# The joint stage of a decoder layer: down sweeps over four token tiles and half the columns, decode steps placed anew, norms once per block

## The reference

```python
p = x @ w_in                                  # q | k | v | forget logits | pooling channels
att  = softmax(q.k/sqrt(d) + c[t] - c[s]) v   # c = cumulative log sigmoid of the forget gates, 8 heads x 64
pool = (trailing mean over 2/4/8/16 - u) @ w_pool * pool_scale
x1 = layer_norm(ALPHA * x + concat(att, pool) @ w_out)
h  = x1 @ w_up + b_up                         # 1024 -> 2 x 2816
hc = b_conv + sum_j h[t-2+j] * w_conv[j]      # causal, width 3, over positions
x2 = layer_norm(ALPHA * x1 + (gelu(hc[:, :2816]) * hc[:, 2816:]) @ w_down)
```

## Time and profile before

| | us |
|---|---|
| median of 3 runs | 3484.64 (3484.43 to 3485.49) |
| profiled execution | 3479.7 |
| its span | 3478.0 |
| joint stage, first up half to last down half | 1313 to 3289 |
| TensorE busy over the span | 3072.4 (88%) |
| VectorE, ScalarE, GpSimd busy | 2131.0, 1707.8, 723.0 |

### The profile page before, as it was taken

One profiled execution on the slowest core, in us unless ns is written; L12 is line 12 of the kernel. 1 busy time (PEld: TensorE's weight loads), 2 busy tenths in 40 slices (PEclk: granted clock), 3 DMA queues, 4 the chain that ended last, 5 costly groups with the idle time before them and its releaser, 6 DMA issues. The chain is left out here.

```text
span 3478.0 us, 57440 instructions
## 1 busy us (share of the span) xinstructions
PE 3072.4 (88%) x19568; PEld 2434.5 (70%) x19568; DVE 2131.0 (61%) x4159; ACT 1707.8 (49%) x3365; POOL 723.0 (21%) x1261
## 2 busy tenths in 40 slices
PE   5999956888887996999899999899998999999767
PEld 5999944776776875777666777677776677777533
DVE  4333434677775655766677566676666776655655
ACT  2111114666664113466446666456664556665445
POOL 0101010000000103233233343233342333322100
PEclk9999977999999998999999999899999999999979
DMA  4443464322203347677887677887777886757575
GB/s 164 127 127 119 119 167 124 71 71 63 68 18 105 125 147 229 206 235 251 284 306 241 219 261 237 284 288 241 247 259 258 298 280 233 255 191 263 180 286 202
DMA packets 287594, 682.11 MB, mean 196 GB/s; under 512 B 57335, under 2 KB 136855, under 8 KB 278815
## 3 DMA queue, kind: packets, MB, share of 16 engines
q1 hardware_dynamic: 191431, 365.36, 32.6%
q0 software_dynamic: 91840, 298.40, 25.1%
q10 hardware_dynamic: 4032, 14.68, 1.2%
HBM read 607.42 MB, written 71.53 MB: 195 GB/s over the span
## 5 line engine op out<-in xcount | busy, mean ns | idle before, releaser
L1436 PE MATMUL F_ps_u<-X_x_hi,F_w_hi 128*128 128x512 f32 x1408 | 579.1, 411 | 7.3 <-DVE F_w_lo L1664 7.3
L1437 PE MATMUL F_ps_u<-X_x_lo,F_w_hi 128*128 128x512 f32 x1408 | 558.2, 396 | 0.0
L1438 PE MATMUL F_ps_u<-X_x_hi,F_w_lo 128*128 128x512 f32 x1408 | 556.4, 395 | 0.0
L1664 DVE TENSOR_TENSOR F_w_lo<-X_raw,F_w_hi 128x512 fp32r<-128x512 f32 x470 | 318.1, 681 | 367.8 <-ACT F_w_hi L1572 367.3
L1572 ACT CAST F_w_hi<-X_raw 128x512 fp32r<-128x512 f32 x470 | 283.7, 613 | 267.6 <-PE F_ps_y L1438 102.5
L1864 POOL DMA_DIRECT2D F_kin<-cache_k x512 | 277.7, 542 | 554.7 <-DVE F_kt L1718 361.1
L1893 POOL DMA_DIRECT2D F_vin<-cache_v x512 | 281.9, 551 | 296.8 <-issue 172.8
L1436 PE MATMUL F_ps_y<-F_w_hi,F_g_hi 128*128 128x512 f32 x704 | 296.5, 421 | 48.9 <-DVE F_w_lo L1664 47.7
L1436 PEld LDWEIGHTS F_ps_u<-X_x_hi,F_w_hi 128*128 128x128 f32 x1408 | 269.4, 191 | 100.2 <-issue 34.8
L1718 DVE STREAM_TRANSPOSE F_kt<-F_kin 128x1024 f32<-128x1024 f32 x256 | 303.6, 1222 | 26.4 <-DMA F_kin<-cache_k 26.3
L1438 PEld LDWEIGHTS F_ps_u<-X_x_hi,F_w_lo 128*128 128x128 f32 x1408 | 268.5, 191 | 60.3
(11 more groups left out here) (291 smaller groups left out, 6070.4 us busy)
## 6 DMA issues: line engine op xcount, KB each, us to landing
F_kin<-cache_k POOLq DMA_DIRECT2D x512, 256.0 KB, 4.5
F_vin<-cache_v POOLq DMA_DIRECT2D x512, 256.0 KB, 4.4
X_raw<-w_up_t SPq DMA_DIRECT2D x118, 512.0 KB, 4.9
X_raw<-w_down SPq DMA_DIRECT2D x117, 512.0 KB, 5.7
F_raw<-w_down SPq DMA_DIRECT2D x59, 512.0 KB, 5.3
F_raw<-w_up_t SPq DMA_DIRECT2D x58, 512.0 KB, 5.2
S_raw<-w_up_t SPq DMA_DIRECT2D x22, 1024.0 KB, 10.3
sc_qk<-A_qk SPq DMA_DIRECT2D x16, 1024.0 KB, 5.1
```

What stands on the lines that cost most here:

```text
L1436: nc.tensor.matmul(out, a_hi, b_hi, start=first, stop=False)
L1437: nc.tensor.matmul(out, a_hi, b_lo, start=False, stop=False)
L1438: return nc.tensor.matmul(out, a_lo, b_hi, start=False, stop=last)
L1664: nc.vector.tensor_tensor(w_lo[:, q % 4, :], raw[q // 2 % RAW][:, q % 2 * 512:(q % 2 + 1) * 512], w_hi[:, q % 4, :].bitcast(F32), ALU.subt ...
```

## The change

- **Down sweep.** `SWEEPS` stays 2 but a sweep now takes all four token tiles (TPB) and one half of the columns. A down half is 4 tiles x 3 matmuls, and there are 44 of them in a block in place of 88. A load of w_down takes two row chunks and 512 columns (512 KB as before), 22 loads a block in place of 44. g is split 512 tokens wide, 44 times a block. The second sweep takes the chunks in the order 18 to 21, 0 to 17, so that the last four chunks of g are free for the second half of the residual (`rows[1]`).
- **Buffers.** A third split buffer of g lies over `h`. `forget` is halved: one unit per load, 64 KB, 256 loads in place of 128. `sums` moves into a kept area.
- **Decode placing.** `decode_places` in place of the list of slots. In an up part a unit starts at a multiple of four halves and takes three of them; in a down part its three steps lie on three consecutive halves. The last step lies on half 524 of 528; it was on 685 of 704.
- **Norms.** `BlockNorm`: the moments of the first column half are taken at the second sweep's start, those of the second at halves 1 and 3 of the next block, then one variance, one root and one inversion for the four rows, and the scaling of a row at halves 7, 9, 11 and 13 in four calls of 512 columns. Two stores a row.
- **Order.** ScalarE casts the weight half q + 4 inside `up_done`, ahead of the gelu. The loads of x are spread over the down part; the residual of a sweep waits tile by tile (`y_done`).

```diff
-    N, TPB, ST, RAW, UN, PARTS = TB, TB // P, 2, 3, NPG // 4, NPG // 4 + 1
-    KR = 3
-    SWEEPS = TPB // ST
-    UPH, DOWNH = 4 * FC, 2 * SWEEPS * FC
+    N, TPB, RAW, UN, PARTS = TB, TB // P, 3, NPG // 4, NPG // 4 + 1
+    KR, GR = 3, 3
+    SWEEPS = D // 512
+    UPH, DOWNH = 4 * FC, SWEEPS * FC
+    LATE = FC - TPB
...
+    def decode_places():
+        at, q = {}, 0
         for s in range(NB + 1):
+            names = ("Q", "R", None) if s == 0 else ("T", "E", "QV") if s < NB else ("T", "V")
             for u in range(UN):
+                if 0 < s and is_up(q):
+                    q += -(q % HB) % 4
+                for name in names:
+                    at[q] = (name, s if name in ("Q", "R", "QV") else s - 1, u)
+                    q += 1
+            if is_up(q):
+                q += -(q % HB) % 4
             for x in ((1, 2, 3, 4) if s < NB else (1, 2)):
+                at[q] = ("X", s, x)
+                q += 1
...
+        g_hi_h = nc.alloc_sbuf_tensor_at("F_g_hi_h", [P, N], F32R, offset=over_h)
+        rows = [r[:, :, :], g[:, LATE:FC, :]]
...
+        X_LOAD_AT, X_SPLIT_AT = (4, 7, 10, 13), (FC + 1, FC + 4, FC + 7, FC + 10)
+        R_LOAD_AT, R_LATE_AT = 15, FC + 8
+        MOMENTS_AT, ROOT_AT, SCALE_AT = (1, 3), 5, (7, 9, 11, 13)
...
+                    k = 2 * (i - 2 * FC)
+                    cols = slice(k // FC * 512, (k // FC + 1) * 512)
+                    src = io["w_down"][0, chunk(k) * P:(chunk(k) + 2) * P, cols].rearrange("(a p) c -> p a c", p=P)
...
+            def down_half(q, b, k):
+                pos, G, (hi, lo) = k % FC, SWEEPS * b + k // FC, g_split(k)
                 pe.wait_ge(lo_done, q + 1)
+                pe.wait_ge(g_lo_done, SWEEPS * FC * b + k + 1)
+                for i in range(TPB):
+                    if pos == 0 and G:
+                        pe.wait_ge(y_read, TPB * (G - 1) + i + 1)
                     toks = slice(i * P, (i + 1) * P)
+                    last = product(ps_y[:, i, :], hi[:, toks], lo[:, toks], w_hi[:, q % 4, :], w_lo[:, q % 4, :],
+                                   pos == 0, pos == FC - 1)
+                    if pos == FC - 1 and i + 1 < TPB:
+                        last.then_inc(y_done, 1)
...
                 nc.scalar.activation(cv[:, gv, :], h[:, gv, 0:N], ACT.Identity, bias=coef[:, f, gv, 4:5],
                                      scale=coef[:, f, gv, 1:2]).then_inc(tap0, 1)
+                if q + 4 < NQ:
+                    high(q + 4)
...
+    def scale_rows(self, dve, link, halves, k):
+        nc = self.nc
         dve.wait_ge(self.rows_in, 32)
+        for w, row in enumerate(halves):
+            last = nc.vector.scalar_tensor_tensor(row, row, self.mv[:, k, 0:1], self.gain[:, w * 512:(w + 1) * 512],
+                                                  ALU.subtract, ALU.mult)
+        link(last)
+        for w, row in enumerate(halves):
+            last = nc.vector.scalar_tensor_tensor(row, row, self.inv[:, k:k + 1], self.shift[:, w * 512:(w + 1) * 512],
+                                                  ALU.mult, ALU.add)
+        last.then_inc(self.gained, 1)
```

More of the change, by code:

```diff
@@ L1245, in __init__, with moments, variance @@
         self.rows_in, self.gained = m.sem("rows_in"), m.sem("gained")
         self.chain = m.sem("norm_chain")
-    def moments(self, dve, link, row, n, k):
+    def moments(self, row, w, k):
+        self.nc.vector.bn_stats(self.stats[:, k, w, :], row).then_inc(self.measured, 1)
+    def variance(self, dve, link, b):
         nc = self.nc
[L1250 to L1259, removed]
+        dve.wait_ge(self.measured, 2 * self.n * (b + 1))
+        for k in range(self.n):
+            aggr = nc.vector.bn_aggr(self.mv[:, k, :], self.stats[:, k, :, :].rearrange("p a b -> p (a b)"))
+            if k + 1 == self.n:
+                link(aggr)
@@ L1260, in scale_row, with take_root, invert @@
+        nc.vector.tensor_scalar(self.var[:, :], self.mv[:, :, 1], EPS, None, ALU.add).then_inc(self.var_ready, 1)
+    def take_root(self, act, b):
+        act.wait_ge(self.var_ready, b + 1)
+        self.nc.scalar.activation(self.root[:, :], self.var[:, :], ACT.Sqrt).then_inc(self.root_ready, 1)
+    def invert(self, dve, link, b):
         nc = self.nc
-        var, root, inv, t1 = (x[:, k:k + 1] for x in (self.var, self.root, self.inv, self.t1))
-        dve.wait_ge(self.root_ready, n + 1)
+        var, root, inv, t1 = (x[:, :] for x in (self.var, self.root, self.inv, self.t1))
+        dve.wait_ge(self.root_ready, b + 1)
@@ L1654, in _ @@
                         exp(s, 0)
-            for k in range(ST):
-                norm.take_root(act, TPB * BLOCKS - ST + k, k)
+            norm.take_root(act, BLOCKS - 1)
         @block.vector
@@ L1821, in _ @@
                         gate(b, FC - 1)
-                    if hf == 0 and f + 2 < SWEEPS * FC:
-                        rest_of_g(SWEEPS * FC * b + f + 2)
-                    if hf == 0 and f in X_SPLIT_AT and b + 1 < BLOCKS:
-                        rest_of_x(b + 1, 2 * X_SPLIT_AT.index(f))
-                    if sweep_end(q):
-                        residual(q)
-                for k in range(ST):
-                    if lag(q, 1 + k):
-                        measure(sweep_of(q - 1 - k), k)
-                    if lag(q, 2 + k):
-                        scale_row(sweep_of(q - 2 - k), k)
+                    if down(q) + 2 < SWEEPS * FC:
+                        rest_of_g(b, down(q) + 2)
+                    if down(q) in X_SPLIT_AT and b + 1 < BLOCKS:
+                        rest_of_x(b + 1, 2 * X_SPLIT_AT.index(down(q)))
+                    if down(q) % FC == FC - 1:
+                        residual(q, b, hf)
+                    if FC <= down(q) < FC + TPB:
+                        measure(b, 0, down(q) - FC)
+                if b and i in MOMENTS_AT:
+                    first = 2 * MOMENTS_AT.index(i)
+                    measure(b - 1, 1, first)
+                    measure(b - 1, 1, first + 1)
+                    if first + 2 == TPB:
+                        norm.variance(dve, norm_links, b - 1)
+                if b and i in SCALE_AT:
+                    if i == SCALE_AT[0]:
+                        norm.invert(dve, norm_links, b - 1)
+                    scale_rows(SCALE_AT.index(i))
                 if q in step_at:
@@ L1913, in _ @@
             for q in range(NQ):
-                for k in range(ST):
-                    if lag(q, 2 + k):
-                        finish(sweep_of(q - 2 - k), k)
+                i = q % HB
+                if q >= HB and i in SCALE_AT:
+                    finish(q // HB - 1, SCALE_AT.index(i))
                 if q in step_at:
```

251 lines of the change are left out of this document (120 added, 131 removed).

## The result

The changed kernel takes 3333.85 us (median of 4 runs, 3330.55 to 3335.91) against 3484.53 before: ratio 0.9567, 95% interval 0.9551 to 0.9584, 151 us less. Forecast were 3371 in a range of 3340 to 3430.

What follows compares the result with a forecast made beforehand. TensorE's matmuls took 1450 of the stage's 1976 us, plus decode units and near 200 of waits, with late w_down in down parts. Parts 301 + 3 x 300 + 3 x 166 + 158 = 1857, +5 at the end: 3371, range 3340 to 3430.

Steps and rivals of the forecast that it cites:

- the price of waits: Joint stage: allowances for waits at block starts and in down parts, 51 us in all.
- Rival D: Joint stage: all waits allowed for (51 us) are absent, 3320 us; chance 0.10.
- Matmuls and units: Down parts: matmuls 123.2 us, 13.3 decode units at 2.48 us, 3 between sequences: 159; last part 155 before waits.
- Up parts: Blocks 2 to 4: 21 groups at 13.27 us plus 14, 293, with allowance 300; first block 295, with allowance 301.
- Late pages: Down parts of blocks 1 to 3: 7 us each for late pages and the residual at a sweep's end; K landing in 5.1.
- The norms at a block start: Start of up parts: scaling, moments and rest of the norm fall into four groups; 7 us allowed, 6 in the first.
- The down part of before: Old down part: low weights late because ScalarE stood 25.8 us for w_down to land; 50.55 MB in 174 us.
- The score addition: Up parts: TensorE's 28 waits before transpose steps, 43.9 us, to go as two halves separate QK and transpose.
- The end: After the last matmul: residual, moments, root, inversion and scaling of four rows, +5 us, bounds +2 and +10.
- A: Down parts: the score-addition wait moves there, 41 units at 1.57 us, 64 us, giving 3435; chance 0.13.
- B: Down parts: transfers stay the bound, 46.4 MB at 244 GB/s, 24 us more three times, giving 3443; chance 0.09.
- C: Down parts: late K pages hold VectorE and then TensorE, 4.3 us a unit, 176 us, giving 3547; chance 0.04.

Runs made afterwards that it cites:

- e10: Changed kernel with the norm's small tiles allocated behind coef, so w_hi and x_hi both lie at 160 past a multiple of 256 bytes: 3315.3 us.
- e11: e10 with g_hi, g_lo and the third split buffer over h also at 160 past a multiple of 256 bytes: 3311.3 us.
- e4: Kernel before the change with the new decode placing alone, w_down still read in both sweeps and norms as before: 3424.2 us.
- e12: e4 with the second sweep's loads of w_down fetching 16 of 1024 columns, all casts, subtractions and matmuls kept: 3406.1 us.
- e7: Changed kernel with two buffers of K pages in place of three: 3473.0 us, ratio 0.9954.
- e6: Changed kernel with four more VectorE passes over each row before it is scaled, 11 us a block: 3372.4 us.
- e5: Changed kernel without the early cast, ScalarE casting weight half q+3 at the head of every half step: 3353.9 us.
- e14: e12 with the four loads of x spread over chunks 2, 4, 6 and 8 of the down part: 3387.4 us.
- e3: Changed kernel with the old decode placing, steps on 7 of 8 up halves and 3 of 4 down halves: 3371.5 us.
- e1: Changed kernel with 32 unused bytes a partition ahead of raw2, w_hi and w_lo: 3328.4 us.
- e8: Kernel before the change with 32 unused bytes ahead of raw2 and the sums tile in the kept area: 3493.9 us, ratio 1.0037.
- e9: Changed kernel with 32 unused bytes ahead of x and 32 ahead of raw2: 3328.7 us.
- e15: Changed kernel with all four loads of x issued one after the other at down half 7: 3334.5 us.

## Why the prediction was wrong

**The step that failed** is the price of waits: 7 us a block start (6 for the first), 7 a down part, 3 for the last, 51 in all. They were measured at about none: in blocks 2 to 4 TensorE stands 0.2 us in an up part and 1.5 in a down part. Rival D, without them, had 3320 and a chance of 0.10. From its stage of 1806 us one comes to the measured 1827 with one term that nobody had named: 4224 up matmuls at a mean pitch of 234.2 ns and not 228.9 are 22 us. (Two smaller ones cancel: 5 us more in the first up part, 6 less in the down parts.) The two errors went against each other; without the second the time would have been further below the range. e10 and e11 show the term by taking it out: their stages take 1806 and 1804 us. The remaining 7 us between 3371 and 3334 are outside the stage's sum: 1.5 at its start, 1.5 at its end, and 4 because I added 4.9 us from the profiled run to the median, which was 0.9 for the changed kernel.

Point by point:
- Matmuls and units: down part without allowance forecast 159.2, measured 158.8, 157.2 and 157.0; last 155, measured 153.6. Right; the unit's price from an undisturbed stretch holds when units lie three halves apart.
- Up parts: forecast without allowance 293, measured 298.2, of which the pitch is 5.6 (1056 matmuls at 5.3 ns): no wait. The first: 295 against 306.1, short by the pitch (5.6) and by some 5 us more. There the clock is at its lower level for 18 us of the stage's first 32, which my prices, all taken at a clock of 1.00, left out; the first query load took 8.0 us and not 10.7.
- Late pages (in the 7 of a down part): K lands in 4.1 and not 5.1. Fewer bytes of w_down do this by themselves: from e4 to e12 the landing in a down part goes from 5.4 to 4.4. e7 shows that the margin is one buffer.
- The norms at a block start: no wait came, but by some 4 us only (e6), and only with the early cast, which I had given no price and which is worth 20 us (e5). I was right by an edit that I had not weighed.
- The down part of before: I held w_down's transfers for its bound, from ScalarE's waits for them. That reading was wrong in the main. Of the 47.7 us of the earlier trace rows that TensorE waited for a low part, 29 are row norms at sweep ends and 15 follow the burst of x, which stood ahead of w_down in SyncE's queue. With the old sweeps and the new placing (e4, e12 to e14) the three causes cost some 6 us a part for the second reading, 6 for the burst and 8 for the norms at the middle sweep end.
- The score addition: its waits went, as said, but put back on the old slots they come to 10 us and not 44 (e3). So I take most of their price for what stood on VectorE ahead of them; that is not shown by itself.
- The end: +3.5 us, forecast +5. The bias loads of 64 KB landed in 3.0 us over the run where 128 KB took 3.3, but in a down part in 3.7 to 3.9 where 128 KB took 3.2 to 3.3; TensorE waited for none. The 32 us that I had estimated by the Trainium skill (DMA: Bandwidth & Descriptors, Bandwidth), and left out of the sum, did not come: they held only if transfers bound the down part, and they don't. Its DMA share is 0.82 to 0.84, as before, and all waits for bias loads together are 1.6 us of VectorE.
- Rivals A, B and C: no wait for the score addition in down parts, no late w_down, 281 to 288 GB/s as in the forecast's 280.

Not tried: the norms once per block alone, on the old sweeps, so the single reading and the norms are priced only by e12 and e14, not apart in the changed kernel. And the third split buffer over h costs 1.5 us a block (F_g_lo_h above), the one place where its wait is reached.

## What to carry to other kernels

When a schedule is made even, take the price of its steps from undisturbed stretches and do not add the old waits back in part. The longest work between two releases either fits the cushion, and the wait is nil, or it does not, and then nearly all that is over comes through, with a slower clock behind a long wait on top (11 us of work over a cushion of 4 cost 9). Count, for each engine, the longest run between two things that the bound engine needs (6.6 us of norms and root against halves of 1.4, or of 2.8), not its mean load, and follow it through the other engines: here VectorE's moments held ScalarE's cast. A long wait on a loaded queue need not be its price: about the same 11 us of issues cost 6 us a part with 8 us of work in flight and none with 17.

## What the runs showed of the hardware

- The start-to-start time of fp32r matmuls of 512 columns hangs on where the tiles lie in SBUF. At a clock of 1.00, with the same instructions, the median was 227, 232 or 234 ns as w_hi moved by 32 to 160 bytes against x_hi; a group of four up halves without a wait took most often 13.27 us in e11 and in the kernel before, 13.46 or 13.47 in e1, e8 and e9, 13.53 in the changed kernel. Over the stage that is 22 us, 0.7% of the run. Small tiles allocated ahead of large operands set it.
- Four issues of 512 KB of x, one behind the other, kept SyncE's queue for 9 to 11 us in e12, 8 to 11 in e15 and 6 to 10 in the kernel before, and the load or two of w_down behind them for 4.4 (e12) and up to 6.5 us (e15) more; spread, each took 0.5 to 0.8 (changed kernel). Whether it is their short pieces or the number under way was not separated.
- In the joint stage the granted clock fell behind waits of TensorE and rose again when it had work: in e5 a wait of 2.7 us had 3.4 us at the lower level with it, in e6 one of 5.4 and in e14 one of 4.9 had 6.8. The four waits of 1.5 us in the changed kernel had none.
